# Nine of twelve wide weight slabs multiplied as plain fp32 instead of as three rounded products

## The chip, the cores and the metric

One Trainium2 chip, of which the kernel uses one core. The metric is the device time of one launch in microseconds (us). Three runs of the kernel before took 1018.0 to 1018.72 us, median 1018.48 us.

## The reference

A decoder trunk of two layers on a sequence of 256 tokens with 2048 features, all in fp32. Cut to the part that matters here, layer 0:

```python
c_act = jax.nn.silu(c)
mod = c_act @ ada_w[l] + ada_b[l]                      # 2048 x 6144
shift, scl, gate_res = jnp.split(mod[:, None, :], 3, axis=-1)
h = _rms(x, norm_g[l]) * (1.0 + scl) + shift           # 256 x 2048
z = h @ ev_w_in[e]                                     # 2048 x 6144
u_a, q, k, v, g = jnp.split(z, _offsets(EVEN_WIDTHS), axis=-1)
```

Pooling, attention, a gate and an output product follow; layer 1 has the same frame with other branches. The norm needs `scl` and `shift`, and these need the large vector-matrix product with `ada_w`.

## The kernel before

**Data.** `X` holds x, and later h, transposed: 16 chunks of 128 features by 256 tokens. The projection weights come in 141 slabs of 1 MB, each loaded as two half slabs of 512 KB with 8 tiles of 128x128. There are four places for half slabs in each of three buffers: `raw` (as loaded), `whi` (rounded to fp32r) and `wlo` (the remainder, rounded to fp32r). So a product with full precision is three fp32r matmuls for each tile: whi with hhi, whi with hlo, wlo with hhi. For a half slab, the loader (SP's queue) fills `raw`, ScalarE (ACT) makes `whi` (`hi`, L395 to L400), VectorE (DVE) makes `wlo` (`lo`, L1023 to L1028), and TensorE (PE) multiplies.

**The vector-matrix product with ada_w** isn't done on PE. It is cut into 12 pieces of 16 units; a unit is 512 KB, 128x1024. DVE multiplies each unit by a scalar for each partition and adds it into `acc` (`add_units`, L1038). PE then sums `acc` over the partitions (`reduce_piece`, L761), DVE adds the bias (`keep_piece`), and the piece is there. The buffer `ada` has four places, and the load of unit n waits until unit n-4 has been added (L254). The units of piece 3 are laid out so that its first half is finished after 8 units (`half_units`, L1048, two half-sized operations for each unit); there are 64 units in pieces 0 to 3.

**The wide stage** (the first 165 us of the span). Four chunks of h depend on one piece: piece 0 gives chunks 0 to 3, piece 1 chunks 4 to 7, piece 2 chunks 8 to 11; the halves of piece 3 give chunks 12, 13 and 14, 15. As h comes chunk by chunk, the first 12 slabs are laid out "wide": `wide_chunk` (L714) multiplies one chunk of h with 12 tiles and adds into 12 half banks of PSUM. So 16 chunks take 192 tiles, 12 slabs. A group of four chunks takes 48 tiles, three slabs, six half slabs.

**Order on DVE**, written out by hand in L1266 to L1298. For piece p = 0, 1, 2: four units; for p > 0 `group_of_h(p-1)` (bias, gain, norm of four chunks, and hlo of each); four units; `lo` of slab 3p-1; four units; `lo` of slab 3p; two units; `lo` of slab 3p+1; two units. After piece 0's units comes the reciprocal root for the norm (L1279 to L1283). Then the units of piece 3, with group 2 of h behind the first four of them, and `lo` of slabs 8 to 11 between them.

**Order on SP's queue** (L265 to L270), which runs strictly in order: for each piece four units, a slab, four units, a slab, four units, a slab, four units. A half slab's load waits for the `lo` of the half slab two slabs earlier (L261), which is the last reader of its place in `raw`.

**Order on ACT** (L515 to L525): four chunks of hhi (`upper_h`), then `hi` of the next slabs, which waits until PE has used the half slab two slabs earlier (L399, semaphore `pe_half`).

**Order on PE** (L879 to L898): for each piece some unused fp32 matmuls (`keep_warm`) from the moment that 12 of its units are added, the reduction, and then the four chunks, each when its hlo is there. For chunks 12 and 13 the first half of piece 3 is needed, for 14 and 15 all of it.

After the wide stage every slab is multiplied with all 16 chunks (`slab`, L696), with loads, `hi` and `lo` two slabs ahead.

Of the kernel before, what the change touches and what calls it, by code (L numbers as in the profile page):

```python
# [5 lines left out]
F32 = mybir.dt.float32  # L6
F32R = mybir.dt.float32r
ALU = mybir.AluOpType
# [40 lines left out]
H_PIECE = {0: (0, 1, 2, 3), 1: (4, 5, 8, 9)}  # L49
GATE = {0: 6, 1: 10}  # L50
WIDE = (12, 8)


C_C = 0
# [40 lines left out]
def build(nc, xT, params, pool_w, w_slabs, ada_units, x1_dram, outT):  # L95
    ctx = ExitStack()
    with ctx:
# [3 lines left out]
        def sem(name):  # L101
            return ctx.enter_context(nc.semaphore(name))
# [77 lines left out]
        q_read = sem("q_read")  # L180
        s_read = sem("s_read")
        xr_done = sem("xr_done")
        hhi_done = sem("hhi_done")
        hlo_done = sem("hlo_done")
        qk_stat = sem("qk_stat")
# [30 lines left out]
        def now(w, t):  # L216
            return w if t is None else w + 2 * t
# [24 lines left out]

        @block.sync
        def _(sp):
            sp.sem_inc(lo_done, 4)
            sp.sem_inc(ada_done, 4)
            sp.dma_start(par[:], params).then_inc(par_in, 16)
            sp.dma_start(X[:], xT).then_inc(x_in, 16)

            def load_units(n, count, t):  # L250
                for u in range(count):
                    slot = (n + u) % 4
                    unit = n + u if t is None else n + u + 4 * t
                    sp.wait_ge(ada_done, unit + 1)  # L254
                    sp.dma_start(ada[:, slot, :], ada_units[bass.ds(unit, 1)].rearrange("a p n -> p (a n)"))\
                      .then_inc(ada_in[slot], 16)

            def load_slab(w, t):
                for half in range(2):
                    slot = half_slot(w, half)  # L260
                    sp.wait_ge(lo_done, 2 * now(w, t) + half + 1)  # L261
                    sp.dma_start(raw[:, slot], w_slabs[bass.ds(now(w, t), 1), :, 8 * half:8 * half + 8, :]
                                 .rearrange("a p k n -> p (a k) n")).then_inc(raw_in[slot], 16)

            for p in range(4):  # L265
                for part in range(4):
                    load_units(UNITS * p + 4 * part, 4, None)
                    if part < 3 and 3 * p - 1 + part >= 0:
                        load_slab(3 * p - 1 + part, None)
            load_slab(WIDE[0] - 1, None)  # L270


            def step(w, t):
                load_slab(w + AHEAD, t)
                load_units(*units_at(w), t)

            for w0, w1 in ((10, 34), (34, 48), (48, 62), (62, 72), (72, 110), (110, 125), (125, 131),
                           (131, 132), (132, N_SLABS - AHEAD)):
                if w0 in (34, 62, 110, 131):
                    for w in range(w0, w1):  # L280
                        step(w, None)
                else:
                    run(sp, w0, w1, step)
# [101 lines left out]
        @block.scalar  # L385
        def _(act):
            act.sem_inc(pe_half, 4)
            n = [0]

            def own(ins):  # L390
# [4 lines left out]
            def hi(w, t, halves=(0, 1)):  # L395
                for half in halves:
                    slot = half_slot(w, half)
                    act.wait_ge(raw_in[slot], 16 * half_uses(w, half, t))
                    act.wait_ge(pe_half, 2 * now(w, t) + half + 1)  # L399
                    act.activation(whi[:, slot], raw[:, slot], ACT.Copy).then_inc(hi_done, 1)  # L400

            def product(w, t):
# [6 lines left out]
            def square_x(i, j):  # L409
                if i >= 2:  # L410
                    act.wait_ge(stat_done, i - 1)
                act.activation(T[:, i % 2, :], X[:, j, :], ACT.Square).then_inc(sq_done, 1)

            def upper_h(layer, chunks):
                for j in chunks:
                    col = shift_col(layer, j)
                    act.wait_ge(xr_done, KC * layer + j + 1)
                    act.activation(hhi[:, j, :], X[:, j, :], ACT.Identity, bias=mod[:, col:col + 1])\
                        .then_inc(hhi_done, 1)
# [86 lines left out]
            act.wait_ge(x_in, 16)  # L506
            for j in range(KC):
                square_x(j, j)
            hi(0, None)
            hi(1, None)  # L510
            root(0, QT)
            act.wait_ge(spread, 1)
            act.activation(DS[:, 0, 0:SEQ], XB[:, 0:SEQ], ACT.Copy).then_inc(r_copied, 1)

            for g in range(3):  # L515
                upper_h(0, range(GROUP * g, GROUP * (g + 1)))
                hi(3 * g + 2, None)
                hi(3 * g + 3, None)
                if g < 2:
                    hi(3 * g + 4, None)  # L520
            upper_h(0, range(12, 14))
            hi(10, None)
            upper_h(0, range(14, 16))
            hi(11, None)
            hi(12, None)  # L525
            act.wait_ge(pe_half, 2 * WIDE[0] + 4)
            for s in range(8):
                read = act.activation(U[:, s, PAD:PAD + SEQ], wide(s), ACT.Copy)
                if s < 4:
                    read.then_inc(z_free[s // 2], 3)  # L530
                else:
                    read.then_inc(s_read, 1)
                if s == 1:
                    hi(13, None)
# [151 lines left out]
        def _(pe):  # L686
# [27 lines left out]
            def wide_chunk(layer, w0, c):  # L714

                pe.wait_ge(hlo_done, KC * layer + c + 1)
                count = WIDE[layer]
                for s in range(count):
                    half, k = (count * c + s) // 8, (count * c + s) % 8
                    slot = half_slot(w0, half)  # L720
                    if s == 0 or k == 0:
                        pe.wait_ge(lo_done, 2 * w0 + half + 1 + 4)

                    mm(wide(s), whi[:, slot, k, :], hhi[:, c, :], start=(c == 0 and s % 2 == 0), stop=False,  # L724
                       skip_group_check=True)
                    mm(wide(s), whi[:, slot, k, :], hlo[:, c, :], start=False, stop=False, skip_group_check=True)  # L726
                    last = mm(wide(s), wlo[:, slot, k, :], hhi[:, c, :], start=False, stop=(c == KC - 1),  # L727
                              skip_group_check=True)
                    if k == 7:
                        last.then_inc(pe_half, 1)  # L730

            def slab_h(w, t):
                slab(w, t, hhi, hlo)

# [144 lines left out]
            for p in range(3):  # L879
                if p:  # L880
                    pe.wait_ge(ada_done, UNITS * p + 12 + 4)
                    keep_warm(24, M)
                reduce_piece(p)
                for c in range(GROUP * p, GROUP * (p + 1)):
                    if c == 11:
                        pe.wait_ge(ada_done, UNITS * 3 + 8 + 4)
                        pe.wait_ge(mod_done, 3)
                        for j in range(4):
                            ins = reduce_part(3, j, half=True)
                        ins.then_inc(half_sum, 1)  # L890
                    wide_chunk(0, U0, c)
            wide_chunk(0, U0, 12)
            wide_chunk(0, U0, 13)
            pe.wait_ge(ada_done, UNITS * 4 + 4)
# [118 lines left out]
        def _(dve):  # L1013
# [9 lines left out]
            def lo(w, t, halves=(0, 1)):  # L1023
                for half in halves:
                    s = half_slot(w, half)
                    dve.wait_ge(hi_done, 2 * now(w, t) + half + 1)
                    dve.tensor_tensor(wlo[:, s], raw[:, s], whi[:, s].bitcast(F32), ALU.subtract)\  # L1027
                        .then_inc(lo_done, 1)  # L1028
# [79 lines left out]
            def lower_h(layer, j):  # L1108
                col = shift_col(layer, j)
                dve.wait_ge(xr_done, KC * layer + j + 1)  # L1110
                dve.wait_ge(hhi_done, KC * layer + j + 1)
                dve.scalar_tensor_tensor(hlo[:, j, :], X[:, j, :], mod[:, col:col + 1],  # L1112
                                         hhi[:, j, :].bitcast(F32), ALU.add, ALU.subtract).then_inc(hlo_done, 1)

# [151 lines left out]
            for p in range(3):  # L1266
                dve.wait_ge(acc_zero, p + 1)
                add_units(UNITS * p, 4, None)
                if p:
                    group_of_h(p - 1)  # L1270
                add_units(UNITS * p + 4, 4, None)
                if p:
                    lo(3 * p - 1, None)
                add_units(UNITS * p + 8, 4, None)
                lo(3 * p, None)
                add_units(UNITS * p + 12, 2, None)
                lo(3 * p + 1, None)
                add_units(UNITS * p + 14, 2, None)
                if p == 0:  # L1279
                    dve.wait_ge(stat_done, KC)  # L1280
                    rsqrt(0, QT, M[:, 0:QT], D_MODEL)
                    token_diag()
                    dve.wait_ge(r_copied, 1)  # L1283
# [1 line left out]
            half_units(48, 4)  # L1285
            group_of_h(2)
            half_units(52, 4)
            lo(8, None)
            half_units(56, 4)
            lo(9, None)  # L1290
            first_half()
# [309 lines left out]
```

## Time and profile before

| what | value |
|---|---|
| median of 3 runs | 1018.48 us |
| the profiled execution | 1017.85 us, its span 1016.1 us |
| PE busy | 955.8 us, 94% of the span |
| DVE busy | 835.2 us, 82% |
| ACT busy | 437.3 us, 43% |
| read from HBM | 256.07 MB |

The profiled execution is 1.75 us longer than its span, and 0.63 us below the median. A matmul's busy time overlaps with the next one's, so the distance between two starts, not the duration, is what one costs. The code has 16 fp32 matmuls in line 789 and 8 in line 999; the trace has 32 and 16 records for them. A record of such a line is one of the two passes of an fp32 matmul. An fp32r matmul has one record.

### The profile page before, as it was taken

The page shows a single profiled execution, that of the slowest core. Times are in us where ns is not written, and L with a number is a line of the kernel's source. Part 1 is how long each engine was busy: PE and PEld are TensorE (multiplying, and loading weights), DVE is VectorE, ACT ScalarE, POOL GpSimd, SP SyncE. Part 2 cuts the span into 40 slices and gives each one's busy share as a digit, 9 for nine tenths or more (in the row PEclk, how much of TensorE's full clock was granted, in tenths as well). Part 3 has the DMA queues.
Part 4 walks back from the last instruction along what each step waited for, and adds up shares of the span by engine and source line. Part 5 has one row for each costly group of instructions (what it writes and reads, how often), then busy time and mean ns, then how long its engine had stood idle before and what let it go on. Part 6 is the DMA issues. An engine that isn't in the chain of part 4 may idle for free.

```text
span 1016.1 us, 20238 instructions
## 1 busy us (share of the span) xinstructions
PE 955.8 (94%) x7728; PEld 945.8 (93%) x7728; DVE 835.2 (82%) x1244; ACT 437.3 (43%) x693; POOL 46.7 (5%) x63
## 2 busy tenths in 40 slices
PE   5197799999999999999999999999999999999997
PEld 5197789999999999999999999999999999999997
DVE  4898987987899778887877898888999986878842
ACT  4122125434555444333344444444446555743331
POOL 1000000011010000000000000000010100000000
PEclk9997798999999999999999999999999999999999
DMA  8999988989777888899857755544445555588961
GB/s 337 339 325 360 324 296 316 321 287 369 290 275 243 279 285 287 312 359 362 312 189 269 242 196 180 189 137 162 150 162 180 167 172 199 196 309 307 342 220 41
DMA packets 71094, 261.32 MB, mean 257 GB/s; under 512 B 7904, under 2 KB 8032, under 8 KB 70768
## 3 DMA queue, kind: packets, MB, share of 16 engines
q1 hardware_dynamic: 68544, 250.86, 70.0%
q0 software_dynamic: 2480, 9.50, 2.6%
q8 instruction: 47, 0.77, 0.3%
q14 instruction: 23, 0.19, 0.1%
HBM read 256.07 MB, written 4.19 MB: 256 GB/s over the span
## 4 chain that ended last, share of the span: by engine, by line
PE 77%; DVE 14%; DMA 4%; issue 3%; ACT 2%; SPq 0%; DVEq 0%; POOL 0%; ACTq 0%; POOLq 0%
PE bank L707 20%; PE bank L708 19%; PE bank L709 19%; DVE acc L1038 6%; DVE wlo L1027 3%; PE bank L809 3%; DMA ada<-ada_units 3%; PE bank L812 3%; PE bank L811 3%; PE bank L724 1%; PE bank L726 1%; PE bank L727 1%; PE bank L777 1%; DVE X L1105 1%; ACT whi L400 1%
## 5 line engine op out<-in xcount | busy, mean ns | idle before, releaser
L400 ACT ACTIVATE whi<-raw 128x1024 fp32r<-128x1024 f32 x282 | 297.2, 1060 | 447.6 <-PE bank L709 338.5
L1027 DVE TENSOR_TENSOR wlo<-raw,whi 128x1024 fp32r<-128x1024 f32 x282 | 341.4, 1224 | 91.9 <-ACT whi L400 91.3
L707 PE MATMUL bank<-hhi,whi 128*128 128x256 f32 x1168 | 337.1, 289 | 2.3 <-ACT T L619 0.9
L708 PE MATMUL bank<-hlo,whi 128*128 128x256 f32 x1168 | 330.4, 283 | 0.0
L709 PE MATMUL bank<-hhi,wlo 128*128 128x256 f32 x1168 | 330.3, 283 | 0.0
L1038 DVE SCALAR_TENSOR_TENSOR acc<-ada,cact,acc 128x1024 f32<-128x1024 f32 x176 | 226.1, 1285 | 33.0 <-DMA ada<-ada_units 16.5
L707 PEld LDWEIGHTS bank<-hhi,whi 128*128 128x128 f32 x1168 | 223.9, 192 | 5.7 <-issue 3.8
L708 PEld LDWEIGHTS bank<-hlo,whi 128*128 128x128 f32 x1168 | 224.1, 192 | 0.1
L709 PEld LDWEIGHTS bank<-hhi,wlo 128*128 128x128 f32 x1168 | 223.8, 192 | 0.0
L707 PE MATMUL bank<-ghi,whi 128*128 128x256 f32 x512 | 147.9, 289 | 0.0
L708 PE MATMUL bank<-glo,whi 128*128 128x256 f32 x512 | 144.9, 283 | 0.0
L709 PE MATMUL bank<-ghi,wlo 128*128 128x256 f32 x512 | 144.8, 283 | 0.0
L724 PE MATMUL bank<-hhi,whi 128*128 128x256 f32 x320 | 95.9, 300 | 20.5 <-DVE hlo L1112 20.5
L1238 DVE SCALAR_TENSOR_TENSOR Y<-U,par,Y 128x256 f32<-128x256 f32 x240 | 98.6, 480 | 0.0
L707 PEld LDWEIGHTS bank<-ghi,whi 128*128 128x128 f32 x512 | 98.3, 192 | 0.0
L708 PEld LDWEIGHTS bank<-glo,whi 128*128 128x128 f32 x512 | 98.3, 192 | 0.0
L709 PEld LDWEIGHTS bank<-ghi,wlo 128*128 128x128 f32 x512 | 98.2, 192 | 0.0
L726 PE MATMUL bank<-hlo,whi 128*128 128x256 f32 x320 | 94.7, 296 | 0.0
L727 PE MATMUL bank<-hhi,wlo 128*128 128x256 f32 x320 | 94.4, 295 | 0.0
L724 PEld LDWEIGHTS bank<-hhi,whi 128*128 128x128 f32 x320 | 65.8, 206 | 21.1 <-DVE hlo L1112 21.1
L809 PE MATMUL bank<-whi,hhi 128*128 128x256 f32 x256 | 73.8, 288 | 0.0
L812 PE MATMUL bank<-wlo,hhi 128*128 128x256 f32 x256 | 72.4, 283 | 0.0
(166 smaller groups left out, 1070.1 us busy)
## 6 DMA issues: line engine op xcount, KB each, us to landing
raw<-w_slabs SPq DMA_DIRECT2D x282, 512.0 KB, 4.9
ada<-ada_units SPq DMA_DIRECT2D x192, 512.0 KB, 6.3
X<-xT SPq DMA_DIRECT2D x1, 2048.0 KB, 7.6
x_dram<-X POOLq DMA_DIRECT2D x4, 512.0 KB, 5.4
outT<-X POOLq DMA_DIRECT2D x4, 512.0 KB, 5.0
V<-pool_w POOLq DMA_DIRECT2D x1, 1024.0 KB, 6.2
U<-xT POOLq DMA_DIRECT2D x2, 512.0 KB, 9.8
V<-xT POOLq DMA_DIRECT2D x2, 512.0 KB, 7.4
```

What stands on the lines that cost most here:

```text
L400: act.activation(whi[:, slot], raw[:, slot], ACT.Copy).then_inc(hi_done, 1)
L707: mm(out, whi[:, s, k, :], ahi[:, c, :], start=(c == 0), stop=False)
L708: mm(out, whi[:, s, k, :], alo[:, c, :], start=False, stop=False)
L709: last = mm(out, wlo[:, s, k, :], ahi[:, c, :], start=False, stop=(c == KC - 1))
L724: mm(wide(s), whi[:, slot, k, :], hhi[:, c, :], start=(c == 0 and s % 2 == 0), stop=False, skip_group_check=True)
L726: mm(wide(s), whi[:, slot, k, :], hlo[:, c, :], start=False, stop=False, skip_group_check=True)
L727: last = mm(wide(s), wlo[:, slot, k, :], hhi[:, c, :], start=False, stop=(c == KC - 1), skip_group_check=True)
L809: mm(out, hhi[:, c, tokens], upper, start=(c == 0 and q == 0), stop=False, skip_group_check=True)
L812: last = mm(out, hhi[:, c, tokens], lower, start=False, stop=(c == KC - 1), skip_group_check=True)
L1027: dve.tensor_tensor(wlo[:, s], raw[:, s], whi[:, s].bitcast(F32), ALU.subtract)\
L1038: dve.scalar_tensor_tensor(acc[:, p % 2, :], ada[:, slot, :], cact[:, bass.ds(k, 1)], acc[:, p % 2, :], ALU.mult, ALU.add).then_inc(ada_do ...
L1238: ins = dve.scalar_tensor_tensor(Y[:, j, :], U[:, j, k:k + SEQ], par[:, wcol:wcol + 1], Y[:, j, :], ALU.mult, ALU.add)
```

## The change

Chunks 0 to 11, that is slabs 0 to 8, are multiplied unsplit: `raw` with `X` itself, in one fp32 matmul for each tile. For these slabs `hi` and `lo` are gone. A half slab of slabs 2 to 10 is now loaded when PE has used the half slab two slabs earlier (`pe_half`); slab 11's load still waits for `lo` of slab 9. ACT makes h in `X` in place and then rounds it to hhi, since later slabs need hhi and hlo of all chunks. SP's queue has another order of units and slabs.

```diff
+UNSPLIT = 9
@@ block.sync
-            sp.sem_inc(lo_done, 4)
+            sp.sem_inc(lo_done, 4 + 2 * UNSPLIT)
@@ load_slab
-                    sp.wait_ge(lo_done, 2 * now(w, t) + half + 1)
+                    if w >= UNSPLIT + 2:
+                        sp.wait_ge(lo_done, 2 * now(w, t) + half + 1)
+                    elif w >= 2:
+                        sp.wait_ge(pe_half, 2 * w + half + 1)
@@
-            for p in range(4):
-                for part in range(4):
-                    load_units(UNITS * p + 4 * part, 4, None)
-                    if part < 3 and 3 * p - 1 + part >= 0:
-                        load_slab(3 * p - 1 + part, None)
+            load_units(0, 8, None)
+            load_slab(0, None)
+            load_units(8, 4, None)
+            load_slab(1, None)
+            load_units(12, 4, None)
+            for p in range(1, 4):
+                load_units(UNITS * p, 8, None)
+                load_slab(3 * p - 1, None)
+                load_units(UNITS * p + 8, 3, None)
+                load_slab(3 * p, None)
+                load_units(UNITS * p + 11, 4, None)
+                load_slab(3 * p + 1, None)
+                load_units(UNITS * p + 15, 1, None)
             load_slab(WIDE[0] - 1, None)
@@ block.scalar
+            act.sem_inc(hi_done, 2 * UNSPLIT)
@@ hi
-                    act.wait_ge(pe_half, 2 * now(w, t) + half + 1)
+                    if w >= UNSPLIT + 2:
+                        act.wait_ge(pe_half, 2 * now(w, t) + half + 1)
+            def full_h(chunks):
+                for j in chunks:
+                    col = shift_col(0, j)
+                    act.wait_ge(xr_done, j + 1)
+                    act.activation(X[:, j, :], X[:, j, :], ACT.Identity, bias=mod[:, col:col + 1])\
+                       .then_inc(h_done, 1)
+                    act.wait_ge(h_done, j + 1)
+                    act.activation(hhi[:, j, :], X[:, j, :], ACT.Copy).then_inc(hhi_done, 1)
@@
-            hi(0, None)
-            hi(1, None)
...
-            for g in range(3):
-                upper_h(0, range(GROUP * g, GROUP * (g + 1)))
-                hi(3 * g + 2, None)
-                hi(3 * g + 3, None)
-                if g < 2:
-                    hi(3 * g + 4, None)
+            full_h(range(0, 12))
+            hi(9, None)
...
             act.wait_ge(pe_half, 2 * WIDE[0] + 4)
+            act.wait_ge(hlo_done, KC)
@@ block.tensor
+            def unsplit_chunk(c):
+                pe.wait_ge(h_done, c + 1)
+                for s in range(WIDE[0]):
+                    half, k = (WIDE[0] * c + s) // 8, (WIDE[0] * c + s) % 8
+                    slot = half_slot(0, half)
+                    if s == 0 or k == 0:
+                        pe.wait_ge(raw_in[slot], 16 * half_uses(0, half, None))
+                    last = mm(wide(s), raw[:, slot, k, :], X[:, c, :], start=(c == 0 and s % 2 == 0), stop=False,
+                              skip_group_check=True)
+                    if k == 7:
+                        last.then_inc(pe_half, 1)
...
-                    wide_chunk(0, U0, c)
+                    unsplit_chunk(c)
@@ block.vector, lower_h
+                if layer == 0 and j < 12:
+                    dve.tensor_tensor(hlo[:, j, :], X[:, j, :], hhi[:, j, :].bitcast(F32), ALU.subtract)\
+                       .then_inc(hlo_done, 1)
+                    return
@@
                 add_units(UNITS * p + 4, 4, None)
-                if p:
-                    lo(3 * p - 1, None)
                 add_units(UNITS * p + 8, 4, None)
-                lo(3 * p, None)
-                add_units(UNITS * p + 12, 2, None)
-                lo(3 * p + 1, None)
-                add_units(UNITS * p + 14, 2, None)
+                add_units(UNITS * p + 12, 4, None)
...
             half_units(52, 4)
-            lo(8, None)
             half_units(56, 4)
             lo(9, None)
```

## Rows read from the trace of the kernel before

**Rows 1.** Stretches: length; PE, PEld, DVE, ACT, POOL busy (count); clock, DMA share, GB/s.
```profile
20.00:40.00 20.00, 3.30 (x16) 3.21 (x16) 16.62 (x14) 6.69 (x8) 0.00 (x0) 1.00 0.95 371
40.00:165.00 125.00, 100.46 (x740) 99.17 (x740) 107.95 (x138) 31.29 (x43) 4.43 (x5) 0.89 0.92 325
165.00:400.00 235.00, 233.87 (x1908) 230.89 (x1909) 199.78 (x268) 116.83 (x213) 17.18 (x18) 1.00 0.82 292
```

**Rows 2.** Timeline of PE: start and length in us, instruction, idle time before.
```profile
51.10 0.58 PE L724 MATMUL bank<-hhi,whi 128*128 128x256 f32 x1 [4.75 <-DVE hlo L1112]
85.25 0.58 PE L724 MATMUL bank<-hhi,whi 128*128 128x256 f32 x1 [6.40 <-DVE hlo L1112]
119.63 0.58 PE L724 MATMUL bank<-hhi,whi 128*128 128x256 f32 x1 [6.63 <-DVE hlo L1112]
```

**Rows 3.** The chain that ended last: start and length in us, what.
```profile
140.81 0.39 PE bank L724
...
149.70 1.04 PE bank L761 x8
...
152.82 0.58 PE bank L724
...
164.63 0.39 ACT U L528
```

**Rows 4.** Groups by line, 0 to 230 us: busy us, mean ns, idle before.
```profile
L1038 DVE SCALAR_TENSOR_TENSOR acc<-ada,cact,acc 128x1024 f32<-128x1024 f32 x70 | 90.1, 1287 | 16.9 <-DMA ada<-ada_units 10.6 <-ACT DS L513 1.7 <-DVE acc L1038 0.2
L1027 DVE TENSOR_TENSOR wlo<-raw,whi 128x1024 fp32r<-128x1024 f32 x45 | 53.8, 1220 | 11.3 <-ACT whi L400 11.3
```

**Rows 5.** Timeline of DVE and ACT: end of piece 0; before groups 1 and 2.
```profile
40.18 0.15 DVE L1083 TENSOR_SCALAR st<-bank 128x2 f32<-128x2 f32 x1
...
81.93 1.28 DVE L1038 SCALAR_TENSOR_TENSOR acc<-ada,cact,acc 128x1024 f32<-128x1024 f32 x1 [0.88 <-DMA ada<-ada_units]
83.13 0.16 DVE L1062 TENSOR_TENSOR mod<-bank,par 128x8 f32<-128x8 f32 x1
...
111.13 0.75 DVE L1055 SCALAR_TENSOR_TENSOR acc<-ada,cact,acc 128x512 f32<-128x512 f32 x1
...
117.51 0.16 DVE L1062 TENSOR_TENSOR mod<-bank,par 128x8 f32<-128x8 f32 x1
84.05 1.31 ACT L418 ACTIVATE hhi<-X,mod 128x256 fp32r<-128x256 f32 x3 [12.01 <-DVE X L1105]
```

**Rows 6.** Waits of SP's queue, 40 to 165 us: total us, times, longest.
```profile
SPq L255 <- DVE acc L1038: 49.4, 32, 3.6
SPq L262 <- DVE wlo L1027: 24.7, 13, 6.5
```

**Rows 7.** Timeline of PE: fp32r matmuls; fp32 passes; last: group's busy, mean ns.
```profile
57.04 0.28 PE L724 MATMUL bank<-hhi,whi 128*128 128x256 f32 x1
57.16 0.28 PE L726 MATMUL bank<-hlo,whi 128*128 128x256 f32 x1
199.15 1.97 PE L789 MATMUL bank<-Y,V 128*128 128x256 f32 x8
821.62 3.62 PE L999 MATMUL bank<-Y,ones 128*128 128x256 f32 x16
...
L999 PE MATMUL bank<-Y,ones 128*128 128x256 f32 x16 | 3.6, 379 | 0.0
```

**Rows 8.** Stretches with the clock of PE, columns as in rows 1.
```profile
85.00:90.00 5.00, 4.75 (x22) 4.75 (x23) 4.69 (x8) 0.86 (x2) 0.00 (x0) 0.50 1.03 420
90.00:95.00 5.00, 5.00 (x42) 5.00 (x42) 3.66 (x4) 2.12 (x2) 0.00 (x0) 0.96 1.04 413
153.00:158.00 5.00, 5.00 (x24) 5.00 (x25) 4.61 (x5) 2.42 (x3) 0.00 (x0) 0.50 0.98 346
```

**Rows 9.** Loads of half slabs: landing times, 40 to 165 us; and one awaited by ACT.
```profile
DMA to landing us min/median/max: 3.3/6.5/9.2
31.44 1.06 ACT L400 ACTIVATE whi<-raw 128x1024 fp32r<-128x1024 f32 x1 [0.21 <-DMA raw<-w_slabs]
```

More of the change, by code:

```diff
@@ L182, in build @@
         xr_done = sem("xr_done")
+        h_done = sem("h_done")
         hhi_done = sem("hhi_done")
```

## The prediction

> **What bounds the kernel now.** I read the busy times first, which stand in the table above: PE is the busiest engine. Then the stretches [rows 1]: from 165 us on PE is busy all but 1.1 of 235 us, so behind the wide stage every microsecond is PE's, and a change of the wide stage's end moves the end of the kernel by as much. In the wide stage PE is busy 100.5 of 125 us at a mean clock of 0.89, while DVE has 108 us of work and the DMA engines are 92% busy. So the stage is where PE waits, and the change touches nothing behind it.
>
> The starts of PE show the rhythm [rows 2, 3]: group 0 starts at 51.10, group 1 at 85.25, group 2 at 119.63, chunk 12 at 140.81, chunk 14 at 152.82, and ACT reads the wide result at 164.63. The periods are 34.15 and 34.38 us. Before each group PE had been idle (4.75, 6.40, 6.63 us), until DVE's hlo. I call the start of group p S(p). What sets S(1) is DVE [rows 4, 5]: sixteen units at about 1.385 us from start to start (1.287 us each and a gap), six `lo` at 1.22 us, the four chunks of h with bias and gain (about 3.7 us from the bias on), together 33.2, and about 1 us of waits for `hi`; the last unit before the bias starts at 81.93, the bias at 83.13, PE at 85.25. SP's queue waits for DVE's adds and for `lo` [rows 6], never for PE. Its own load isn't far below its limit: a period moves 22 transfers of 0.524 MB, 11.5 MB, in 34 us.
>
> **Price of the new product.** Two fp32r matmuls start 0.12 us apart [rows 7], so a tile cost 3 x 0.12 = 0.36 us. An fp32 tile has two passes. Line 999: 16 passes in 3.62 us, less the last one's 0.379, is 15 distances of 0.216. Line 789, whose weights also change from pass to pass: (1.97 - 0.38)/7 = 0.227. I take 0.22, so 0.44 us for a tile, bounds 0.43 and 0.455. The change spares DVE and ACT and costs PE 0.08 us x 144 tiles = 11.5 us; the question is whether PE's idle time hides it.
>
> A rule speaks against the change here: the Trainium skill, FP8 and Floating Point Precision, TensorE Precision Notes, says that true fp32 takes four passes through the array. The trace shows two records per matmul, each nearly as far from the next as two fp32r ones, so it can hold both numbers; which of them is the price, rival C asks.
>
> At half the clock [rows 8] 22 fp32r matmuls take 4.75 us, 0.216 each, and the clock rises near 90.2, 5 us after the start. An fp32r pass cold costs what an fp32 pass costs warm, so an fp32 pass cold should cost 0.427 and a tile 0.85. I take 5.1 us for it; the start in the third row of this group stays cold for all of its 5 us, so up to 6 is possible. In the first 5.1 us of a group 6 tiles are done, the rest at 0.44. The six half slabs (8 tiles each) of a group are used up at S + 6.0, 9.5, 13.0, 16.5, 20.0 and 23.6 us.
>
> **Group 0.** The four `lo` before 40 us go. The second half of slab 1 landed by 31.44 [rows 9]; the units 12 to 15 behind it follow at about 1.35 us each, so the last lands near 36.8 and is added by 38.1, 2.1 us sooner than the 40.2 of before [rows 5]. PE now waits for h, not for hlo: ACT's first operation started at 84.05 [rows 5], takes 0.5, so PE could start at 84.6, not 85.25: 0.65 us. S(0) moves by -2.75, to 48.35 (bounds -0.65 and -4.7, the four `lo` whole). `hi` and `lo` are otherwise work that others hid or waited for; ACT's extra copy for each chunk takes some 0.5 us, DVE's group takes about 1.5 us more for it, and both lie inside gaps worked out below. The subtraction that makes hlo has one operand less and the same size, priced at nothing. `hi` of slab 9 stands behind all twelve chunks on ACT and is free when group 2's h is made, before slab 9 lands. ACT's new wait for the sixteenth hlo comes 10 us after that hlo: nothing. POOL's queue isn't touched.
>
> **Periods 1 and 2: the queue waits for PE.** Before, `raw` was only a stop: its places came free with `lo`, and whi and wlo held two slabs more. Now a place comes free when PE is done, and SP's queue holds all units behind that wait. In period 1: units 16 to 23 go out before and around S; slab 2 waits for S+6.0 and S+9.5. Units 24 to 26 stand behind it, so nothing is issued from about S to S+6 and DVE, done with unit 23 near S+9, waits for unit 24 until about S+14. A half slab lands at the earliest 3.3 us after its issue [rows 9], at the median 6.5 behind others; alone in the queue it is nearest to the first. The others come behind it every 1.3 to 1.4 (0.524 MB at 371 to 400 GB/s). So slab 2's second half lands at S+12.9, and the twelve transfers behind it (units 24 to 26, slab 3, units 27 to 30, slab 4, unit 31) at 1.35 each bring unit 31 at S+29.1; slab 4's second half, issued at S+23.6, would allow S+28.5, so both limits meet. I take S+29.2. From there it is DVE: units 31 to 34, 4 x 1.385 us, unit 35 starts at S+34.7 (its load, issued when unit 31 is added, at S+30.6, lands in 3.3 to 4.1, in time), the bias 1.2 us later, PE 1.5 us behind that: S(1) = S(0)+37.4 = 85.7, against 85.25. What is late next is thus unit 31, no longer `lo`.
>
> Period 2 ends with units 47 and 48 to 51: unit 47 starts at S+29.2, the four half-laid units take 117.51 - 111.13 = 6.4 us [rows 5], so the bias is at S+29.2+1.4+6.4 = S+37.0 and S(2) = S(1)+38.5 = 124.2, against 119.63: +4.6.
>
> **Chunks 12 to 15.** Unit 59 stands behind slab 9, whose second half waits for S(2)+16.5; it lands at S+21.2 and is added by S+22.9. Then `lo` of slab 9 (2.35 us), bias and gain (0.4), two norms, hhi and hlo: chunk 12 starts at S(2)+27.2 = 151.4. Before it was 140.81-119.63 = 21.2 behind S(2). That is +6.0, in all +10.6. PE was done with group 2 at S+24.1, so it idles 3 us. Before chunk 14 it idled 152.82 - 150.74 = 2.1 us and then ran at 0.50 [rows 3, 8]; I take cold: the 24 tiles take 5.1 + 16 x 0.36 = 10.8 us where they took 8.8: +2.0, in all +12.6. DVE's path beside it (units 60 to 63, `lo` of slab 10) takes 9.1 us, and is covered by PE's 10.8. If the clock holds, DVE's path is what ends it, at +10.9 in all. From there (149.70 on) nothing differs, slab 11 having been loaded since about S+29.
>
> **Sum:** -2.75 + 3.25 + 4.1 + 6.0 + 2.0 = +12.6 us. The profiled execution took 1017.85, 0.63 below the median, so 1030.5 us.
>
> A second rule bears on the clock: the Trainium skill, TensorE: Matmul & The Clock Gate, Why this matters for your kernels, advises no idle gaps over about 3 us between bursts. The trace has a cold start after 2.1 us. By the rule the start of chunk 12 stands at its edge and may be warm; then the sum would be 1028.8.
>
> **The rivals.**
> A. PE stays at full clock through the groups' starts. Each group ends 2.5 us sooner, and with it the wait of the queue: 3 x 2.5 us, and the 2.0 of chunk 12, off the sum: 1021. Against: PE still idles about 4.8 us before S(1) and S(2), like the 4.75 us before 51.10. For: the keep-warm matmuls come later. Chance 0.08.
> B. On the other side: the relief of DVE decides. The six `lo` and the waits for `hi` were 8 to 10 us of each period. If unit 31 lands before S+25.9, the period is below 34.15; at a floor of 11.5 MB by the 371 GB/s of 20 to 40 us [rows 1] a period is 31.1 us: -3 twice, -2.75 for group 0 and -2 behind group 2 give about 1007. It needs the last wait of slab 4 at S+20, so an fp32 tile of 0.36 or less, below both rows. Chance 0.06.
> C. The fp32 tile is dearer than both rows, as in four fp32r distances: 0.48. Each group takes 1.7 us more, 5 in all: 1036. Line 789 allows 0.455, which is +2. Chance 0.12. (The Trainium skill's four passes, named above, would give this case if each cost as much as an fp32r matmul of this kernel.)
> D. The fp32 matmuls don't raise the clock. Then a group takes 48 x 0.85 = 41 us, 17 more each: 1083. Against: the passes of lines 789 and 999 [rows 7] run at full clock, though they didn't have to raise it. Chance 0.03.
> E. The change does less than it says: with the new queue order the waits for PE are met before SP reaches them, and nothing moves but group 0: 1016 to 1019. Against: slab 2 is reached when PE has only begun. Chance 0.04.
>
> **Chances.** The forecast itself has 0.67. The range reaches from A, 1021.5, to 1037, which takes in C and slower landings (4.5 us in place of 3.3 adds about 1 us a period); outside are B, D, E. A measurement here can tell 0.2%, 2 us, from no change. Faster: B and part of E, 0.07. Same: most of E and the low edge of A, 0.04. Slower: 0.89.
>
> **What the profile after should show.** Passes of the new line 0.216 to 0.227 apart, 288 of them. SP's waits for PE instead of for `lo`, longest near 6 us. DVE idle until DMA ada in each period, first about 5 us. Starts near 48.3, 85.7, 124 and 151.4, end of the wide stage near 177. Behind it the distances as before. If S(1) is at 83 or earlier, the step of the queue is wrong; if the passes are apart by other than 0.22, the price is.

## The result, and the profile after

The changed kernel took 1035.72 us (median of 4 runs, 1034.31 to 1036.82), the kernel before 1018.24 us (4 runs, 1016.66 to 1018.72). The ratio is 1.0182, 95% interval 1.0162 to 1.0201: slower by 17.5 us. The profiled execution after took 1034.31 us with a span of 1032.5 us, 16.4 us more than the span of before. The forecast was 1030.5 us, range 1021.5 to 1037.

Busy times on the page after:

```profile
PE 967.1 (94%) x7584; PEld 947.5 (92%) x7584; DVE 815.7 (79%) x1226; ACT 422.9 (41%) x687; POOL 46.7 (5%) x63
```

DVE lost 19.5 us of work and ACT 14.4, PE gained 11.3: that is the exchange the change makes. The stretches (columns as in [rows 1]), the wide stage being longer now:

```profile
40.00:165.00 125.00, 97.61 (x478) 86.71 (x479) 81.26 (x108) 15.54 (x32) 2.85 (x3) 0.89 0.77 281
165.00:180.00 15.00, 12.90 (x110) 12.81 (x109) 10.50 (x15) 4.82 (x6) 1.58 (x2) 1.00 0.76 257
180.00:415.00 235.00, 233.14 (x1902) 229.97 (x1901) 198.28 (x267) 116.28 (x212) 17.18 (x18) 1.00 0.81 297
```

Against [rows 1]: from 40 to 165 us DVE has 81 us of work in place of 108, PE isn't busier (97.6 against 100.5), and the DMA share fell from 0.92 to 0.77. All three have room, and the stage is longer. So something serial replaced them. Behind the stage PE is as full as before.

Starts of PE (timeline of PE, idle time before in brackets; they answer to [rows 2, 3]):

```profile
49.98 23.48 PE L761 MATMUL bank<-X,raw 128*128 128x256 f32 x96 [4.10 <-ACT X L435]
89.28 22.61 PE L761 MATMUL bank<-X,raw 128*128 128x256 f32 x96 [4.52 <-ACT X L435]
128.92 18.09 PE L761 MATMUL bank<-X,raw 128*128 128x256 f32 x72 [5.99 <-ACT X L435]
158.29 0.58 PE L745 MATMUL bank<-hhi,whi 128*128 128x256 f32 x1 [5.21 <-DVE hlo L1150]
172.69 0.39 PE L745 MATMUL bank<-hhi,whi 128*128 128x256 f32 x1 [2.10 <-DVE hlo L1150]
```

The periods are 39.30 and 39.64 us, where they were 34.15 and 34.38. The chain that ended last shows what took DVE's place in them:

```profile
49.98 16.59 PE bank L761 x64
66.59 0.33 SPq L269
66.96 5.80 DMA ada<-ada_units
72.78 1.29 DVE acc L1072
74.17 1.30 DVE acc L1072
75.48 6.88 DMA ada<-ada_units
82.44 1.29 DVE acc L1072
```

PE uses up the fourth half slab, only then does SP issue the second half of slab 3 (L269), only then a unit (27), which lands 5.8 us later; when DVE has added it and the next one, which frees a place, the load of unit 32 may start, and lands 6.9 us later. The waits of SP's queue, 40 to 180 us, against [rows 6] (the stage ends some 17 us later here, so the stretch is longer):

```profile
SPq L269 <- PE bank L761: 55.1, 18, 7.3
SPq L259 <- DVE acc L1072: 29.1, 23, 4.3
SPq L269 <- DVE wlo L1061: 17.5, 6, 8.9
```

55 us of SP's time are waits for PE, one for each of the 18 half slabs 4 to 21 that wait for it. What that does to the transfers stands in two-us stretches just behind S(0) (columns as in [rows 1]):

```profile
52.00:54.00 2.00, 2.00 (x7) 1.55 (x6) 1.40 (x3) 0.89 (x3) 0.00 (x0) 1.00 0.27 107
54.00:56.00 2.00, 2.00 (x8) 1.72 (x7) 1.90 (x2) 0.00 (x0) 0.00 (x0) 1.00 0.00 0
56.00:58.00 2.00, 2.00 (x11) 1.74 (x11) 1.79 (x3) 0.00 (x0) 0.00 (x0) 1.00 0.38 137
58.00:60.00 2.00, 2.00 (x11) 1.77 (x10) 0.81 (x1) 0.00 (x0) 0.00 (x0) 1.00 0.33 125
```

The DMA engines stand still from 54 to 56 us, and are more than 60% idle in each of the four stretches. DVE follows (timeline of DVE): it waits for units 24, 27, 31 and 32.

```profile
64.77 1.28 DVE L1072 SCALAR_TENSOR_TENSOR acc<-ada,cact,acc 128x1024 f32<-128x1024 f32 x1 [5.96 <-DMA ada<-ada_units]
...
72.78 5.45 DVE L1072 SCALAR_TENSOR_TENSOR acc<-ada,cact,acc 128x1024 f32<-128x1024 f32 x4 [3.79 <-DMA ada<-ada_units]
80.40 1.28 DVE L1072 SCALAR_TENSOR_TENSOR acc<-ada,cact,acc 128x1024 f32<-128x1024 f32 x1 [2.16 <-DMA ada<-ada_units]
82.44 5.45 DVE L1072 SCALAR_TENSOR_TENSOR acc<-ada,cact,acc 128x1024 f32<-128x1024 f32 x4 [0.76 <-DMA ada<-ada_units]
87.81 0.16 DVE L1096 TENSOR_TENSOR mod<-bank,par 128x8 f32<-128x8 f32 x1
```

### The profile page after: what moved, and what is told of

Read it like the earlier page. It is cut to its first block, busy times and chain, and to the rows that moved or that the text cites. A ratio compares the mean times of both kernels' runs of the same rounds, so it can differ in the third digit from the quotient of the medians.

```text
span 1032.5 us, 19905 instructions
## 1 busy us (share of the span) xinstructions
PE 967.1 (94%) x7584; PEld 947.5 (92%) x7584; DVE 815.7 (79%) x1226; ACT 422.9 (41%) x687; POOL 46.7 (5%) x63
## 4 chain that ended last, share of the span: by engine, by line
PE 84%; DVE 8%; DMA 5%; ACT 1%; issue 1%; SPq 0%; DVEq 0%; POOL 0%; ACTq 0%; POOLq 0%
PE bank L728 20%; PE bank L729 18%; PE bank L730 18%; DMA ada<-ada_units 5%; PE bank L761 5%; DVE acc L1072 3%; PE bank L843 3%; PE bank L846 3%; PE bank L845 3%; PE bank L745 2%; PE bank L748 2%; PE bank L747 2%; DVE wlo L1061 1%; PE bank L795 1%; PE bank L811 1%; PE bank L774 1%
## 5 line engine op out<-in xcount | busy, mean ns | idle before, releaser
L417 ACT ACTIVATE whi<-raw 128x1024 fp32r<-128x1024 f32 x264 | 278.3, 1060 | 420.6 <-PE bank L730 342.8
L1061 DVE TENSOR_TENSOR wlo<-raw,whi 128x1024 fp32r<-128x1024 f32 x264 | 320.0, 1223 | 87.5 <-ACT whi L417 86.7
L728 PE MATMUL bank<-hhi,whi 128*128 128x256 f32 x1168 | 337.3, 289 | 1.7 <-ACT T L640 0.9
L729 PE MATMUL bank<-hlo,whi 128*128 128x256 f32 x1168 | 330.7, 283 | 0.0
L730 PE MATMUL bank<-hhi,wlo 128*128 128x256 f32 x1168 | 330.6, 283 | 0.0
L728 PEld LDWEIGHTS bank<-hhi,whi 128*128 128x128 f32 x1168 | 224.1, 192 | 4.9 <-issue 3.8
L761 PE MATMUL bank<-X,raw 128*128 128x256 f32 x288 | 69.6, 407 | 14.6 <-ACT X L435 14.6
L761 PEld LDWEIGHTS bank<-X,raw 128*128 128x128 f32 x288 | 59.0, 206 | 23.9 <-ACT X L435 14.9
L845 PE MATMUL bank<-whi,hlo 128*128 128x256 f32 x256 | 72.5, 283 | 0.0
L745 PE MATMUL bank<-hhi,whi 128*128 128x256 f32 x176 | 51.5, 293 | 7.3 <-DVE hlo L1150 7.3
```

What stands on the lines that cost most here:

```text
L728: mm(out, whi[:, s, k, :], ahi[:, c, :], start=(c == 0), stop=False)
L729: mm(out, whi[:, s, k, :], alo[:, c, :], start=False, stop=False)
L730: last = mm(out, wlo[:, s, k, :], ahi[:, c, :], start=False, stop=(c == KC - 1))
L761: last = mm(wide(s), raw[:, slot, k, :], X[:, c, :], start=(c == 0 and s % 2 == 0), stop=False, skip_group_check=True)
L845: mm(out, hlo[:, c, tokens], upper, start=False, stop=False, skip_group_check=True)
```

## The experiments

Three theories. **Q**: the loss is the wait of SP's queue for PE. **P**: it is PE's higher price for the fp32 tiles. **O**: it is the new order in the queue. Before and after differ in all three, so the first runs split them. All times are medians with the ratio to the kernel before and its 95% interval; the kernel before had 1017.2 to 1018.3 us beside them. Differences to the changed kernel are taken between medians of different sets of runs.

### The order alone

```diff
 (the kernel before)
-            for p in range(4):
-                for part in range(4): ...
+            load_units(0, 8, None)
+            load_slab(0, None)
+            ... as in the change
```

> The kernel before with the new order of units and slabs on SP's queue alone; all products stay split and the loads still wait for lo. Theory Q (the loss comes from SP's queue waiting for PE): the order alone costs or gives little, 1016 to 1021 us. Theory P (the loss is the price of the fp32 matmuls on PE, 0.08 us x 144 tiles): the same, 1018. If the order itself were the cause (theory O), most of the 17 us would show here: over 1028.

1022.06 us, ratio 1.0037 (1.0021 to 1.0053). The order costs 3.8 us with split products, above the upper end of my 1016 to 1021, and far from the 17. So O is a small part, if it adds at all in the changed kernel.

### The wait for PE without the fp32 matmuls

```diff
 (e1_order)
-                    sp.wait_ge(lo_done, 2 * now(w, t) + half + 1)
+                    if 2 <= w <= 10:
+                        sp.wait_ge(pe_half, 2 * w + half + 1)
+                    else:
+                        sp.wait_ge(lo_done, 2 * now(w, t) + half + 1)
```

> As e1_order, and the loads of slabs 2 to 10 wait for PE as in the changed kernel, but the products stay split at 0.36 us a tile. Theory Q: the half slabs are used up at about S+5, 8, 11, 14, 17 and 19.5, unit 31 lands near S+26, and a period takes 35 to 36 us against 34.15: 1020 to 1024. Theory P: nothing, 1018.

1037.97 us, ratio 1.0199 (1.0168 to 1.0229). With no fp32 matmul at all, the wait costs 15.9 us over e1_order, as much as the whole change. Its waits of SP's queue:

```profile
SPq L265 <- PE bank L738: 38.3, 14, 6.8
SPq L265 <- DVE wlo L1038: 17.1, 6, 8.4
```

P alone is refuted, and my number for Q (1020 to 1024) was far too low, which matters below: PE used the half slabs up faster here (0.36 us a tile), and the period was still 91.34 - 51.17 = 40.2 us. Its DVE shows why: it stands idle before two `lo` (below), which wait for `hi` of slab 2, once more before unit 27 (2.4 us, until 71.98), and then still has four `lo` and eight adds to do before the bias at 89.22.

```profile
60.33 1.23 DVE L1038 TENSOR_TENSOR wlo<-raw,whi 128x1024 fp32r<-128x1024 f32 x1 [2.26 <-ACT whi L411]
64.35 1.23 DVE L1038 TENSOR_TENSOR wlo<-raw,whi 128x1024 fp32r<-128x1024 f32 x1 [2.79 <-ACT whi L411]
```

### The fp32 matmuls without the wait

Eight places for half slabs; every second pair of slabs goes into V and Y, which nothing uses before the wide stage is over.

```diff
 (the changed kernel, load_slab; unsplit_chunk reads from the same places)
-                    elif w >= 2:
+                    elif w == UNSPLIT + 1:
                         sp.wait_ge(pe_half, 2 * w + half + 1)
+                    elif w >= 4:
+                        sp.wait_ge(pe_half, 2 * w + half - 3)
+                    if w < UNSPLIT and (2 * w + half) % 8 >= 4:
+                        sp.dma_start(far(slot), ...).then_inc(far_in[slot], 16)
+                        continue
```

> The changed kernel with eight places for half slabs in the unsplit stage instead of four (V and Y, unused until later, hold the other four), so that a load waits for PE four slabs back, not two. The fp32 matmuls stay. Theory Q: SP's queue hardly waits for PE, a period falls to 31 to 34 us, and the time to 1008 to 1020. Theory P: PE's price stays, 1029 or more.

1017.83 us, ratio 0.9990 (0.9976 to 1.0003): 17.9 us below the changed kernel, no difference from the kernel before. All fp32 matmuls are there, so with the wait for PE nearly gone the exchange of `hi` and `lo` for the fp32 price comes out even, and the 17 us are the wait's. The waits for PE went from 55.1 us to

```profile
SPq L281 <- PE bank L775: 7.7, 3, 4.2
```

and the engines kept transferring behind S(0), in the four us that answer to 52 to 56 above:

```profile
51.00:53.00 2.00, 2.00 (x6) 1.56 (x5) 1.38 (x3) 0.92 (x3) 0.00 (x0) 1.00 1.02 389
53.00:55.00 2.00, 2.00 (x9) 1.68 (x8) 1.90 (x2) 0.00 (x0) 0.00 (x0) 1.00 0.93 305
```

But it isn't faster than before either. The starts:

```profile
49.01 16.48 PE L775 MATMUL bank<-X,raw 128*128 128x256 f32 x64 [4.10 <-ACT X L447]
82.64 9.82 PE L775 MATMUL bank<-X,Y 128*128 128x256 f32 x32 [3.21 <-ACT X L447]
117.45 9.48 PE L775 MATMUL bank<-X,V 128*128 128x256 f32 x32 [4.14 <-ACT X L447]
143.18 0.39 PE L757 MATMUL bank<-hhi,whi 128*128 128x256 f32 x1 [1.54 <-DVE hlo L1164]
```

S(0) comes 2.1 us earlier than before and S(2) 2.2: all of that is group 0's, and the two periods together are no shorter than before (68.4 against 68.5 us). DVE, six `lo` lighter in each, waits for units instead, 14.5 us from 40 to 118 us where it waited 0.9.

Chunk 12 comes 25.7 us behind S(2) in place of 21.2 ([rows 2, 3]). It is tempting to call that the price of the fp32 tiles, 48 x 0.08 = 3.8 us, but PE is not what ends last there: it idles 1.54 us before chunk 12, for DVE's hlo. The chain that ended last goes through the load of unit 59, issued when its place came free and 10 us on its way:

```profile
127.32 10.05 DMA ada<-ada_units
137.40 0.76 DVE acc L1103
```

So 25.7 is what unit 59 and DVE behind it give; PE alone would have been ready 24.2 us behind S(2).

### The last unit ahead of the last slab

```diff
-                load_units(UNITS * p + 11, 4, None)
+                load_units(UNITS * p + 11, 5, None)
                 load_slab(3 * p + 1, None)
-                load_units(UNITS * p + 15, 1, None)
```

> The changed kernel with the last unit of each piece (31, 47, 63) ahead of the last slab's load in SP's queue instead of behind it. Theory Q: unit 31 no longer waits for the sixth half slab; it lands some 2 us sooner, behind units 27 to 30, so two periods are 1.5 to 2.5 us shorter: 1030 to 1033 against 1035.7. Theory P: no difference, 1035 to 1036.

1038.49 us, ratio 1.0188 (1.0155 to 1.0221): nothing gained, against what I expected of Q. Timeline of DVE in this kernel:

```profile
73.53 6.83 DVE L1071 SCALAR_TENSOR_TENSOR acc<-ada,cact,acc 128x1024 f32<-128x1024 f32 x5 [5.08 <-DMA ada<-ada_units]
84.16 5.45 DVE L1071 SCALAR_TENSOR_TENSOR acc<-ada,cact,acc 128x1024 f32<-128x1024 f32 x4 [3.80 <-DMA ada<-ada_units]
```

Unit 31 was added by 80.4, 1.3 us sooner. But group 1 needs units 32 to 35 as well (`group_of_h` stands behind them), and these are now the ones behind slab 4. They landed at 84.2 in place of 82.4. In this queue, with the wait where it is, moving one unit ahead of it only puts another that the next group needs behind it.

### No idle time of PE ahead of a group

```diff
                 reduce_piece(p)
+                keep_warm(18 if p else 8, M)
```

> The changed kernel with unused fp32 matmuls between the reduction of a piece and the start of its group (18 before groups 1 and 2, 8 before group 0), so that PE doesn't idle there. Theory Q: if the clock is then full from the group's first tile, a group ends 2.5 us sooner, the queue's waits for PE too, and two or three of these give 1028 to 1031 us. If the clock isn't what holds the queue (or the extra matmuls don't keep it up): 1035 to 1037.

1030.09 us, ratio 1.0106 (1.0062 to 1.0150): 5.6 us below the changed kernel. The clock does take part. It was full from the first tile of group 2 on, and chunk 12 came 154.26 - 127.44 = 26.8 us behind S(2) in place of 29.4. Before group 1 the extra matmuls ran at half the clock, 6.94 us, and S(1) came at 89.67, no earlier than 89.28. But the group itself then ran at full clock from its first tile (25 passes in 5.56 us), and period 2 was 127.44 - 89.67 = 37.8 us in place of 39.6. So a full clock at the start of a group was worth 1.9 and 2.6 us, near the 2.5 that theory Q named.

### Half the PE time with the wait

```diff
-                    last = mm(wide(s), raw[:, slot, k, :], X[:, c, :], ...
+                    n = SEQ if c == 0 else P
+                    last = mm(wide(s)[:, 0:n], raw[:, slot, k, :], X[:, c, 0:n], ...
```

> The changed kernel in which the unsplit matmuls of chunks 1 to 11 multiply only 128 of the 256 tokens (half of this part of the product is left out), so that PE needs half the time for a group and the loads still wait for it. Theory Q: half slabs are used up by S+3.5, 5.3, 7, 9, 11 and 12.5; the queue's waits shrink to a third, the periods to 31 to 35 us, the time to 1005 to 1018. If instead the landing times of the loads, or the order in the queue, held the periods (theory D), they stay above 37 us and the time above 1028.

1024.94 us, ratio 1.0066 (1.0044 to 1.0089). 10.8 us less than the changed kernel, with SP's waits for PE at 24.3 us in place of 55.1. (This kernel leaves out half of the tokens in chunks 1 to 11; chunk 0 keeps all its tokens, so the first half slab of group 0 is used up no faster.) That is in favour of Q, but it lies outside both expectations: PE's group 0 is now 15 us instead of 23.5, below the 48 x 0.36 = 17.3 us that 48 split tiles take even at full clock, and period 1 is still 84.80 - 48.35 = 36.45 us; period 2, where all four chunks are halved, is 122.01 - 84.80 = 37.2. The longest wait stays:

```profile
SPq L269 <- PE bank L762: 24.3, 9, 6.5
```

So the wait isn't only as long as PE's pace makes it. SP reaches slab 2 at about the moment when the group starts, and the first two half slabs behind S fall into a queue that has run dry. That part depends on how deep the places are more than on how fast PE is: e3_deep, with more places, is rid of it. It fits that e2_split_pe_wait cost so much with fast tiles, though that kernel has its `lo` as well, and no run separates the two.

### Depth with the old order, and fewer unsplit slabs

> As e3_deep (eight places, all nine slabs unsplit), but with the order of units and slabs of the kernel before. Theory Q with the order's own cost as e1_order measured it (+3.8 us): 1013 to 1016. If the order is tied to DVE's lo and doesn't matter without it: 1016 to 1019, as e3_deep.

e8_deep_old_order (e3_deep with the loop of the kernel before in SP's queue) took 1019.82 us, ratio 1.0025 (1.0008 to 1.0043). The order's 3.8 us didn't come back. That it is tied to `lo` isn't shown, since here the old order has a hole of its own: slab 10 still waits for the end of group 2, and units 60 to 63 stand behind it. DVE waited 8 us for unit 60:

```profile
145.96 0.75 DVE L1095 SCALAR_TENSOR_TENSOR acc<-ada,cact,acc 128x512 f32<-128x512 f32 x1 [7.97 <-DMA ada<-ada_units]
```

Up to chunk 12 the old order is the better one (timeline of PE):

```profile
140.49 0.47 PE L749 MATMUL bank<-hhi,whi 128*128 128x256 f32 x1
```

Chunk 12 starts 2.7 us earlier than in e3_deep, and PE goes into it without idling, while DVE's first hlo had been ready since 137.6. Here, then, PE is the bound of group 2 with fp32 tiles, and the stretch takes 140.49 - 116.49 = 24.0 us where it took 21.2: 2.8 us more, not 4.5, because before the change DVE ended this stretch, and PE had a little time to spare.

e7_six_deep draws the two conclusions: unsplit only where PE has idle time (groups 0 and 1), and no wait for PE.

```diff
-UNSPLIT = 9
+UNSPLIT = 6
 (slabs 2 to 5 go into V, Y and U; slabs 6 and 7 into raw, long free)
-                    unsplit_chunk(c)
+                    if c < 8:
+                        unsplit_chunk(c)
+                    else:
+                        wide_chunk(0, U0, c)
 (SP's order, and lo of slabs 6 to 8 on DVE, as in the kernel before)
```

> Only the first six slabs (chunks 0 to 7) unsplit, group 2 split as before, places for all of them (raw, V, Y and U), the order of the kernel before. Groups 0 and 1 are shorter on DVE and PE's idle time hides the fp32 price; in group 2, whose end is PE's, the price (e3_deep: chunk 12 starts 25.7 us behind S(2), 21.2 before) isn't paid. Theory Q: 1009 to 1014, faster than the kernel before. Theory P: 0.08 x 96 = 8 us over it, 1026.

1014.99 us, ratio 0.9975 (0.9956 to 0.9995), and once more:

> e7_six_deep once more, beside the two others on the same chip: 1013 to 1016 us, faster than the kernel before by 2 to 4 us.

1013.93 us, ratio 0.9965 (0.9949 to 0.9982). Both intervals are below 1: this version is 2 to 4 us faster than the kernel before and some 21 us faster than the changed one. In e7_six_deep's trace the starts are 49.09, 81.80, 116.95, 138.46: chunk 12 comes 21.5 us behind S(2), as before; the first period is 32.7 us, the second 35.2, and no wait of SP's queue for PE is left. S(0) comes 2.0 us earlier than before, and that is most of the gain: the periods together are 67.9 us against 68.5 (69.2 in e11_six_deep_again), since DVE again waits for units, 9.2 us from 40 to 118 us, 10.6 in e11. The kernel before with more places and all slabs split wasn't run; but the 2.0 us at S(0) can't be the places', because all units of piece 0 and the first two slabs stand ahead of slab 2 in the queue; the four `lo` before it are gone, as in the changed kernel.

```profile
49.09 16.63 PE L777 MATMUL bank<-X,raw 128*128 128x256 f32 x64 [4.10 <-ACT X L445]
81.80 8.74 PE L777 MATMUL bank<-X,Y 128*128 128x256 f32 x32 [2.14 <-ACT X L445]
116.95 0.58 PE L759 MATMUL bank<-hhi,whi 128*128 128x256 f32 x1 [5.57 <-DVE hlo L1169]
138.46 0.39 PE L759 MATMUL bank<-hhi,whi 128*128 128x256 f32 x1 [0.64 <-DVE hlo L1169]
```

### The same with PE kept busy

```diff
+                if p == 2:
+                    keep_warm(18, M)
...
+            keep_warm(8, M)
             wide_chunk(0, U0, 14)
```

> e7_six_deep with unused fp32 matmuls where PE idles on a stretch that PE ends: 18 before group 2 (its idle was 5.6 us) and 8 before chunk 14 (2.1 us). If the clock is then full at both starts, the first saves 2.5 us, the second 0 to 2.5 (chunk 14 started at full clock in some runs already): 1010 to 1013 us. If they don't keep the clock up, 1015.

> The kernel before with the same unused matmuls and nothing else, to tell the clock's gain from that of the unsplit slabs: 1013 to 1016 us. The difference to e9 is then what the six unsplit slabs bring, 2 to 4 us.

e9_six_deep_warm: 1013.35 us, ratio 0.9964 (0.9949 to 0.9979); e10_before_warm: 1016.35 us, ratio 0.9991 (0.9974 to 1.0008). Against e11_six_deep_again (1013.93) the first brings nothing that can be told, and the second is no change. In e9's trace group 2 runs at clock 1.00 (44 matmuls from 116 to 121 us), where e11, whose group starts at 118.14, has 13 matmuls at 0.50 in the same stretch; but the stretch behind it isn't PE's alone there, so little of it reaches the end. Where the waits for PE make the stretch PE's, more of the same matmuls (before all three groups, e5_warm) gave 5.6 us.

## Why the prediction was right or wrong

The sign and the mechanism were right: SP's queue waits for PE, DVE for the units behind that wait. The time lay inside the range, near its top. By the steps (us; the starts of before in [rows 2, 3]):

| step | predicted | measured |
|---|---|---|
| S(0) | -2.75 | -1.1 |
| period 1 | +3.25 | +5.15 |
| period 2 | +4.1 | +5.3 |
| S(2) to chunk 12 | +6.0 | +8.2 |
| chunk 12 to 14 | +2.0 | +2.4 |
| chunk 14 to ACT's read | 0 | -2.6 |
| behind the wide stage | 0 | -0.9 |
| sum | +12.6 | +16.4 (spans) |

**Price of the tile: right.** Eleven passes in the warm part of group 0 take 2.54 us, so (2.54 - 0.379)/10 = 0.216 from start to start, 0.432 a tile; I had taken 0.44. Timeline of PE, with its first record at 59.70:

```profile
59.70 2.54 PE L761 MATMUL bank<-X,raw 128*128 128x256 f32 x11
```

The Trainium skill (FP8 and Floating Point Precision, TensorE Precision Notes) gives true fp32 four passes. The trace agrees only if each of the two records is two of them without a gap, 4 x 0.108; four at the distance of the fp32r matmuls, rival C, is out.

**Group 0: right in kind.** `lo` gone and PE waiting for h (idle until ACT X, not DVE hlo) is what the trace shows. Of the 1.6 us that are missing, 0.9 are the start: PE's first matmul came at 10.45 us, at 9.51 before. In the other kernels with the same code there the first matmul comes at 9.5 to 10.0 and S(0) is 48.4 to 49.3; only e4_unit_first has 10.69 and 49.98.

**The use-up times: right.** I had S+6.0, 9.5, 13.0, 16.5, 20.0, 23.6; the second half of slab 3 went out at 66.59 = S+16.6, that of slab 4 at S+23.5, and the cold tiles cost what was worked out.

**The step that failed is the landing of the units behind the wait**, "at 1.35 each bring unit 31 at S+29.1": it landed at S+30.4, unit 47 at S(1)+30.4, unit 59 at S(2)+23.6 in place of 21.2. I had taken a queue where the first load after a standstill lands in 3.3 us and each other 1.35 us behind the one ahead. The 1.35 held where the engines were full: units 27 and 31, six transfers apart, landed at 72.78 and 80.40, 1.27 us for each. What I had too short was the landing just behind a release: unit 27, by my spacing due at S+21.0, landed at S+22.8, 5.8 us after its issue. Measured from 56 to 84 us, a unit's load took 4.4, 6.6 at the median and 7.5 us at most from issue to landing:

```profile
DMA to landing us min/median/max: 4.4/6.6/7.5
```

I had 4.2 us for unit 59, and got 6.8. The fastest landing in [rows 9], 3.3, was the wrong one to take for it; what came is near the median there, 6.5. Why a load behind a release takes that long no run separates. The misses are 1.2, 1.2 and 2.4 us in three steps. Another 0.75 us of period 1 is unit 32: I had DVE in one piece from unit 31 to 35, but the load of 32 waits for the add of 28 (75.48 in the chain) and landed late too.

**Rival B was weighed with a wrong condition.** I wrote that a tile of 0.36 us or less would turn the sign. e6_half_tokens has DVE's relief and about half of the fp32 price, and is slower than before all the same. (e2_split_pe_wait has 0.36 and is slower too, but it keeps `lo` on DVE and so isn't B's case.) The wait's fixed part (the queue standing empty while the group begins) I had in the text ("nothing is issued from about S to S+6") but not in this rival, where I scaled the whole wait with PE's pace.

**The chunk starts:** chunk 12 started cold after 5.2 us of idle time, as taken. Chunk 14 started at full clock after 2.10 us, with the same idle time at which it was cold before ([rows 8]); this is the -2.6, and I had no term for it. The advice of the Trainium skill (TensorE: Matmul & The Clock Gate, Why this matters for your kernels), no gaps over about 3 us, fits the start of chunk 14 after the change and not the one before.

Rival A (full clock at each start, 1021) is the change with another edit: in e5_warm groups 1 and 2 ran at full clock from their first tile, and the time was 1030.1. By the steps that is 1.9 and 2.6 us, about as A priced them, but chunk 12 still started at 0.50, and S(1) wasn't earlier. D is refuted: groups after the change run at full clock from S+5 on with fp32 matmuls alone. E didn't happen: SP's queue waited 55.1 us for PE.

**Where luck helped.** By the spans the sum was 3.8 us short. Up to chunk 14 it was short by 7.3 us (group 0, both periods, the way to chunk 12 and on to 14); the full clock at chunk 14 and the stretch behind the wide stage, for neither of which I had a term, gave 3.5 us back. Without them the time would have been some 1039 us, by this estimate from the steps, and outside my range. The mechanism is shown, its size was too small.

## What to carry to other kernels

A buffer that is freed later than before can block everything behind its load in the same in-order queue; count what is queued there, and for how long the transfer engines will be empty, before counting what the change saves on an engine. The wait costs even where the freeing engine is fast, because the queue runs dry at each start; more places (here idle buffers) took it away without touching the arithmetic. And trade one engine's time for another's only in stretches where the second has idle time: with groups 0 and 1 unsplit the kernel was 2 to 4 us faster, most of it at S(0); in group 2 PE then was the bound, and the stretch took 2.8 us more. Between them, in the periods, the relief of DVE brought next to nothing: it waited for units instead. Before a stretch is put down to an engine's price, look whether that engine idled at its end.

## What the runs showed of the hardware

- An fp32 matmul of 256 columns is two records 0.216 us apart, also with new weights for each tile: 0.432 us against 3 x 0.12 for three fp32r matmuls. The 0.227 of line 789 [rows 7] didn't come again.
- Fp32 matmuls alone bring the clock up, about 5 us behind the start of a group, as fp32r ones did [rows 8]: after the change it is 0.54 from 88 to 93 us and 1.00 from 93 to 98, with S(1) at 89.28. In group 0 the clock column reads 1.00 throughout, yet 12 passes fit between 50 and 55 us and 25 between 55 and 60: there only the pace shows the slow start.
- PE's clock after the same 2.10 us of idle time was at half in one kernel and full in the other. A sum shouldn't carry such a start as certain; it is worth some 2.5 us here.
- Loads of units issued in a burst after a standstill took 4.4 to 7.5 us to land, 6.6 at the median, where 3.3 to 4.1 was what I had taken for a nearly empty queue. Six transfers of a full queue landed 1.27 us apart.
